# A hybrid decoder trunk on one core: dt's 16 columns leave the unit list, V goes first, the first weights load in halves, and the last unit's split and the final norm weight move forward

## The chip, the cores and the metric

The kernel runs on one core of one Trainium2 chip. The metric is device time in microseconds (us) of one execution; lower is better. Before the change three runs took 965.58 to 969.66 us, median 967.36 us. A change of less than about 0.5% (4.8 us) can't be told from none.

The engines are named as in the profile: PE (TensorE, matrix products), DVE (VectorE), ACT (ScalarE), POOL (GpSimd), SP (SyncE, which here issues nearly all DMAs).

## The reference, cut to what matters

576 tokens (512 of a prompt, 8 sequences of 8 sample tokens) go through two layers of 1024 channels.

```
h    = rmsnorm(x, norm_w)
proj = h @ w_in        # 1024 -> [z 1024 | xBC 1536 | dt 16 | q 512 | k 512 | v 512 | g_ret 512 | u 512 | g_pool 512]
dt   = softplus(dt_raw + dt_bias);  a = -exp(a_log)      # 16 heads
y_ssd  = rmsnorm((ssd(silu(conv(xBC)), dt, a) + x*d_skip) * silu(z))
y_ret  = rmsnorm(retention(rotary(q), rotary(k), v)) * silu(g_ret)
y_pool = pool(u) @ pool_w * pool_scale * silu(g_pool)
x = x + concat(y_ssd, y_ret, y_pool) @ w_out             # 2048 -> 1024
...                                                      # after both layers
y = rmsnorm(x, final_norm_w)
```

The new recurrent states are outputs too. All data are 32-bit floats.

## The kernel before

**Units.** The two projections of a layer are cut into units of 128 output columns. A unit is eight blocks of 128 channels by two halves of 288 tokens by three products (high part of the weights times high and low part of h, low part times high part), so 48 matmuls of 128x288 (`products`, L534 to L536). A layer has 61 units: dt (U_DT = 0, its 16 columns padded with zeros to 128), four each of q, k and v, 12 of conv, 4 pool, 8 gates, 8 z, and 16 of the output projection. The accumulators of two units alternate.

**What a unit needs.** Two units ahead SP loads the raw weights (`load`, L383); ACT writes their high part (`high`, L888), after the unit that used this buffer is projected; DVE subtracts to get the low part (`split`, L1156, semaphore w_split). PE starts a unit when its split is there and the accumulator of the unit two before is read (evac). On ACT and DVE the main loop goes over u and starts each round with the high part, or the split, of unit u+2, so both stand in the queue behind the end of unit u.

**Start of a layer.** x is multiplied with the norm weight and split into high and low (`raw_high`, `raw_low`); the first five units (EARLY) are computed from this, before the root mean square is known, and DVE multiplies them with rstd when it reads them (`read_early`). In the first layer units 0 and 1 run interleaved, four blocks apart, as x arrives (`project_first`). `norm_sum` adds the squares of x over the channels with four plain 32-bit matmuls by a matrix of ones. While units 0 to 3 run DVE and ACT make the scaled h (`scaled`, `half_high`), which later units use.

**dt and rotary on DVE.** dt_raw is read from unit 0 (L1181). In ACT's round 4 come its bias, Abs and Exp (L1063 to L1067); DVE does the rest of softplus and the running sums as `dt_part(0..7)` in rounds 4 to 11 (a RECIPROCAL in part 1), and one q or k unit is rotated in each of rounds 4 to 11 (`rotate`). Part 7 leaves `stacked` (semaphore stk_ok). Behind unit 12 PE transposes it (L862), and DVE copies the result to `token_vecs` in its round 12 (L1611, L1612; semaphore tokv_ok). Retention starts behind unit 13 (`ret_turn`, L691); its first matmuls overwrite the same PSUM banks and wait for tokv_ok.

**The end.** The last two units go half by half (`project_last`), each half with its own final norm: add to x (L1680), square (L1127), sum (L797, L799), rstd (L1134, L1136), and eight SCALAR_TENSOR_TENSOR x * final_norm_w * rstd of 128x288 (`out_of`, L1695). In the last rounds ACT's `high` and DVE's `split` of unit u+2 stand behind the square and the add of round u.

Of the kernel before, what the change touches and what calls it, by code (L numbers as in the profile page):

```python
# [13 lines left out]
P = 128  # L14
# [23 lines left out]
U_DT = 0  # L38
U_Q = 1
U_K = U_Q + RP  # L40
U_V = U_K + RP
U_CONV = U_V + RP
# [7 lines left out]
DT_AT = 4  # L50
# [79 lines left out]
def trunk(nc: bass.Bass, a):  # L130
    with ExitStack() as ctx:
# [69 lines left out]
        stk = place("stacked", [96, TOK])  # L201
        tokv = place("token_vecs", [P, TILES, 96])
        gm = place("scores", [P, GROUPS, CH])
# [54 lines left out]
        tab_in = sem("tables_loaded")  # L258
        vec_in = sem("layer_vectors_loaded", 16)
# [4 lines left out]
        s_st = sem("small_states_loaded", 32)  # L264
        w_hid = sem("w_high", UNITS)
# [94 lines left out]
        sum_half = sem("last_norm_sum")  # L360
        rstd_half = sem("last_norm_rstd")
# [15 lines left out]
        def _(sp):  # L377
# [24 lines left out]
            def beside(l, s):  # L402
# [11 lines left out]
                if s == 9:  # L414
# [5 lines left out]
                if s == 10:  # L420
# [58 lines left out]
            sp.dma_start(vec[:, :], a["vec"][0]).then_inc(vec_in, 16)  # L479
            for i in range(4):  # L480
                sp.dma_start(x[:, 2 * i:2 * i + 2, :], a["x"][:, 2 * i:2 * i + 2, :]).then_inc(s_x[i], 16)
                if i < 2:
                    load(i)
            for l in range(DEPTH):
# [6 lines left out]
                for u in range(UNITS):  # L491
# [8 lines left out]
                    if l + 1 < DEPTH and u == U_OUT + 10:  # L500
                        sp.wait_ge(*of(y_full, KT))
                        sp.dma_start(vec[:, :], a["vec"][l + 1]).then_inc(vec_in, 16)
                    if l + 1 < DEPTH and u in (UNITS - 4, UNITS - 2):
                        keep((u - UNITS + 4) // 2)
                    if l and u in (0, 2):
                        keep(2 + u // 2)
            for half in range(2):
                c = slice(half * HALF, (half + 1) * HALF)
                for i in range(4):
                    sp.wait_ge(f_ok, KT * half + 2 * i + 2)  # L510
# [5 lines left out]
        def _(pe):  # L516
# [20 lines left out]

            def project_first():

                for step in range(KT + LAG):  # L540
                    if step == KT + 2:
                        norm_sum(0)
                    for u, k in ((0, step), (1, step - LAG)):
# [4 lines left out]
                        if k == 0:  # L548
# [6 lines left out]
            def project_again():  # L555

                pe.wait_ge(*of(w_split, 1))
# [226 lines left out]

            def project_last():
# [30 lines left out]
            for l in range(DEPTH):  # L816
# [4 lines left out]
                for u in range(1, UNITS if l + 1 < DEPTH else UNITS - 2):  # L821
# [3 lines left out]
                    if u == S_RST:  # L825
# [27 lines left out]
                    elif u > 1 or l:  # L853
                        project(u)
                    if U_GPOOL < u < U_GPOOL + 4 and (u - S_SSD) % 2 == 1:

                        pool_mm_(u - U_GPOOL - 1)
                    if u == S_STK:
                        pe.wait_ge(*of(tab_in, 16))
                        pe.wait_ge(*of(stk_ok, 1))  # L860
                        for t in range(TILES):
                            mm = pe.transpose(mb[:, t // 4, (t % 4) * 96:(t % 4 + 1) * 96], stk[:, cols(t)] if t < TILES - 1 else gm[0:96, 0, :],  # L862
                                              ident[0:96, 0:96])
                        mm.then_inc(stk_T, 1)
# [12 lines left out]
        def _(eng):  # L877
# [40 lines left out]
            def read_out(u):  # L918

                src = acc_of(whole(l, u))  # L920
                if u < U_V:
# [5 lines left out]
                elif u < U_CONV:  # L927
                    go(act(halves(vT[:, u - U_V, :]), src, ACT.Copy), evac, u + 1)
# [82 lines left out]
            eng.wait_ge(*of(vec_in, 16))  # L1011
            for j in range(KT):
                if j % 2 == 0:
                    eng.wait_ge(*of(s_x[j // 2], 16))
                if j in (1, 4):
                    high(j // 4)
                raw_high(j, 0)
            for j in range(KT):
                if j >= 2:
                    eng.wait_ge(*of(sq_add, j - 1))  # L1020
                square(j, 0)
            for l in range(DEPTH):
                for u in range(UNITS if l + 1 < DEPTH else UNITS - 2):
# [3 lines left out]
                    m = u - U_OUT - OUT_CHUNKS  # L1027
                    if m >= 0:
# [10 lines left out]
                    if whole(l, u) + 2 < DEPTH * UNITS:  # L1039
# [20 lines left out]
                    if u == DT_AT:  # L1060
                        eng.wait_ge(*of(s_par, 48))
                        eng.wait_ge(*of(evac, 1))
# [6 lines left out]
                    if u == 6:  # L1069
# [3 lines left out]
                    if u == 10:  # L1073
# [843 lines left out]
```

## Time and profile before

| | us |
|---|---|
| runs | 965.58, 967.36, 969.66 |
| the profiled execution | 967.27 |
| its span (first to last instruction) | 965.5 |
| PE busy | 947.5 (98%) |
| DVE busy | 693.6 (72%) |
| ACT busy | 419.3 (43%) |
| mean granted TensorE clock | 0.994 of full |

The profile is of one execution. In a row of the timeline the first number is the start, the second the time over which the instructions of the row lie; what stands in brackets is how long the engine was idle before and what released it. A plain 32-bit matmul of the program shows as two MATMUL rows. The starts of matmuls that follow each other show PE's pace; their lengths overlap.

### The profile page before, as it was taken

The page shows a single profiled execution, that of the slowest core. Times are in us where ns is not written, and L with a number is a line of the kernel's source. Part 1 is how long each engine was busy: PE and PEld are TensorE (multiplying, and loading weights), DVE is VectorE, ACT ScalarE, POOL GpSimd, SP SyncE. Part 2 cuts the span into 40 slices and gives each one's busy share as a digit, 9 for nine tenths or more (in the row PEclk, how much of TensorE's full clock was granted, in tenths as well). Part 3 has the DMA queues.
Part 4 walks back from the last instruction along what each step waited for, and adds up shares of the span by engine and source line. Part 5 has one row for each costly group of instructions (what it writes and reads, how often), then busy time and mean ns, then how long its engine had stood idle before and what let it go on. Part 6 is the DMA issues. An engine that isn't in the chain of part 4 may idle for free.

```text
span 965.5 us, 18839 instructions
## 1 busy us (share of the span) xinstructions
PE 947.5 (98%) x7974; PEld 906.6 (94%) x7974; DVE 693.6 (72%) x944; ACT 419.3 (43%) x701; POOL 45.4 (5%) x148
## 2 busy tenths in 40 slices
PE   8999999999999999999999999999999999999996
PEld 7999999999999889999999999999989988899995
DVE  6899677857896568664558967787679757686445
ACT  6432454234775135532334235533267633544222
POOL 0000011010010000000000001011101000000000
PEclk9999999999999999999999999999999999999999
DMA  7234221234234453423333242221533451652222
GB/s 268 104 115 146 81 67 49 69 108 155 88 107 153 153 204 123 142 91 109 132 127 113 87 143 64 67 67 50 157 107 103 136 198 63 224 202 66 88 66 99
DMA packets 38277, 113.33 MB, mean 117 GB/s; under 512 B 11088, under 2 KB 13776, under 8 KB 36784
## 3 DMA queue, kind: packets, MB, share of 16 engines
q1 hardware_dynamic: 37936, 111.23, 34.7%
q8 instruction: 63, 1.03, 0.4%
q0 software_dynamic: 256, 0.88, 0.3%
q14 instruction: 22, 0.18, 0.1%
HBM read 94.63 MB, written 17.47 MB: 116 GB/s over the span
## 4 chain that ended last, share of the span: by engine, by line
PE 90%; DVE 5%; ACT 3%; DMA 1%; issue 1%; SPq 0%; DVEq 0%; ACTq 0%
PE acc L534 26%; PE acc L536 25%; PE acc L535 25%; PE misc L638 2%; PE misc L624 1%; DVE w_lo L1156 1%; ACT w_hi L888 1%; PE misc L691 1%; PE misc L641 1%; DMA x<-in_x 1%; PE misc L713 1%; PE acc L781 1%; PE misc L762 1%; PE misc L732 1%; PE misc L655 1%; PE misc L610 1%
## 5 line engine op out<-in xcount | busy, mean ns | idle before, releaser
L534 PE MATMUL acc<-hin,w_hi 128*128 128x288 f32 x1536 | 461.4, 300 | 0.9 <-DVE w_lo L1156 0.9
L536 PE MATMUL acc<-hin,w_lo 128*128 128x288 f32 x1536 | 453.8, 295 | 0.0
L535 PE MATMUL acc<-hin,w_hi 128*128 128x288 f32 x1536 | 453.7, 295 | 0.0
L534 PEld LDWEIGHTS acc<-hin,w_hi 128*128 128x128 f32 x1536 | 289.5, 188 | 13.6 <-issue 10.8
L888 ACT ACTIVATE w_hi<-w_raw 128x1024 fp32r<-128x1024 f32 x122 | 129.0, 1057 | 381.8 <-PE acc L536 378.6
L535 PEld LDWEIGHTS acc<-hin,w_hi 128*128 128x128 f32 x1536 | 289.5, 188 | 0.4
L536 PEld LDWEIGHTS acc<-hin,w_lo 128*128 128x128 f32 x1536 | 289.5, 188 | 0.0
L1156 DVE TENSOR_TENSOR w_lo<-w_raw,w_hi 128x1024 fp32r<-128x1024 f32 x122 | 148.8, 1220 | 126.5 <-ACT w_hi L888 126.4
L534 PE MATMUL acc<-mix,w_hi 128*128 128x288 f32 x416 | 124.0, 298 | 4.0 <-DVE w_lo L1156 1.7
L536 PE MATMUL acc<-mix,w_lo 128*128 128x288 f32 x416 | 122.6, 295 | 0.0
L535 PE MATMUL acc<-mix,w_hi 128*128 128x288 f32 x416 | 122.5, 294 | 0.0
L534 PEld LDWEIGHTS acc<-mix,w_hi 128*128 128x128 f32 x416 | 78.0, 188 | 4.9 <-issue 3.0
L535 PEld LDWEIGHTS acc<-mix,w_hi 128*128 128x128 f32 x416 | 78.0, 188 | 0.3
L536 PEld LDWEIGHTS acc<-mix,w_lo 128*128 128x128 f32 x416 | 78.1, 188 | 0.0
L1256 DVE SCALAR_TENSOR_TENSOR conv_out<-halo,vec,conv_out 128x600 f32<-128x600 f32 x72 | 60.8, 844 | 2.5
L981 ACT ACTIVATE decay<-decay,token_vecs 128x128 f32<-128x128 f32 (+1 forms) x160 | 47.8, 379 | 1.9
L1587 DVE TENSOR_TENSOR x<-x,acc 128x576 f32<-128x576 f32 x30 | 22.6, 754 | 34.6 <-PE acc L536 32.7
L892 ACT ACTIVATE mix<-x,vec 128x576 fp32r<-128x576 f32 x16 | 11.8, 770 | 38.8 <-DVE x L1587 34.5
L906 ACT ACTIVATE tmp<-x 128x576 f32<-128x576 f32 x22 | 14.8, 678 | 31.8 <-PE acc L536 14.2
L638 PE MATMUL misc<-decay,xdt 128*64 128x128 f32 (+1 forms) x320 | 27.3, 266 | 0.0
L1303 DVE TENSOR_TENSOR xdt<-misc,token_vecs 128x1024 f32<-128x1024 f32 x10 | 12.2, 1224 | 19.1 <-PE misc L615 18.9
L638 PEld LDWEIGHTS misc<-decay,xdt 128*64 128x64 f32 (+1 forms) x320 | 19.4, 136 | 6.8 <-issue 6.8
(212 smaller groups left out, 1045.2 us busy)
## 6 DMA issues: line engine op xcount, KB each, us to landing
w_raw<-in_w SPq DMA_DIRECT2D x122, 512.0 KB, 3.6
decay<-cum_rows SPq DMA_DIRECT2D x8, 1024.0 KB, 6.0
h<-in_ssm SPq DMA_DIRECT2D x16, 512.0 KB, 6.3
out_ssm_s<-h SPq DMA_DIRECT2D x16, 512.0 KB, 6.2
x<-in_x SPq DMA_DIRECT2D x8, 576.0 KB, 6.9
x_kept<-x SPq DMA_DIRECT2D x4, 576.0 KB, 2.8
x<-x_kept SPq DMA_DIRECT2D x4, 576.0 KB, 5.8
out_y<-x SPq DMA_DIRECT2D x8, 288.0 KB, 2.2
```

What stands on the lines that cost most here:

```text
L534: pe.matmul(out, wh, hi, start=k == 0, stop=False)
L535: pe.matmul(out, wh, lo, start=False, stop=False)
L536: return pe.matmul(out, wl, hi, start=False, stop=k == KT - 1)
L638: mm = pe.matmul(dst[r, :], xdt[0:n, h * HD:(h + 1) * HD], decay[0:n, t % 2, h, 0:n], start=True, stop=not inter)
L888: go(act(w_hi[:, unit % 2, :, :], w_raw[:, unit % RAW, :, :], ACT.Copy), w_hid, unit + 1, 0)
L892: go(act(raw_h(0, j), x[:, j, :], ACT.Copy, scale=vec[:, V_NW + j:V_NW + j + 1]), p_hi, j + 1, at)
L906: go(act(tmp[:, j % 2, :], x[:, j, :], ACT.Square), sqd, j + 1, at)
L981: go(act(m, m, ACT.Relu, scale=-1.0, bias=tokv[0:n, t, h:h + 1]))
L1156: go(V.tensor_tensor(w_lo[:, unit % 2, :, :], w_raw[:, unit % RAW, :, :], w_hi[:, unit % 2, :, :].bitcast(F32), ALU.subtract), w_split, un ...
L1256: ins = V.scalar_tensor_tensor(out=o, in0=h[:, c:c + CVO], scalar=w[c], in1=o, op0=ALU.mult, op1=ALU.add)
L1303: go(V.tensor_tensor(heads(xdt[:, :]), src, dt_b, ALU.mult))
L1587: go(V.tensor_tensor(halves(x[:, m, :]), halves(x[:, m, :]), acc_of(whole(l, u)), ALU.add), x_new, o + 1)
```

## The change

- The dt unit goes; a layer has 60 units, V first (units 0 to 3), then q (4 to 7), k (8 to 11), conv from 12. DVE's `read_early` now reads the four v units and the first q unit.
- dt's columns are their own small weights, 8 blocks of 128x32 (`wdt`, in the place of token_vecs), multiplied with the norm weight by one DVE instruction. `dt_parts` multiplies them as plain 32-bit numbers with the raw x, block k into the strip of 32 PSUM partitions k mod 4; ACT copies the four strips out, `dt_folded` adds them with a 0/1 matrix behind unit 2, and DVE scales the result with rstd (`dt_scaled`).
- The dt rounds on ACT and DVE come one round sooner (DT_AT 3 instead of 4; 5 and 9 instead of 6 and 10); rotations stay in rounds 4 to 11, so q or k unit u is now rotated in round u itself.
- `stacked` is turned inside unit 12, after its first three blocks, and retention starts behind unit 12. DVE's copies to token_vecs stay in round 12, behind the split of unit 14.
- In the first layer the first unit's weights load in two halves, and two squares and their adds move ahead of the second unit's high part and split.
- In the last layer the last unit's high part and split come before the x add of unit 57 (the third from the end); ACT multiplies x with the final norm weight as soon as a chunk is done, and DVE's output step is four TENSOR_TENSOR of 128x2x288 per half instead of eight SCALAR_TENSOR_TENSOR of 128x288.

DVE around the token vectors, before (the rotation of the last k unit, part 7 of dt, the split of unit 14, the copies, the split of unit 15, retention):

```order
L1273 TENSOR_TENSOR qk<-qk,conv_out 128x576 [waits vector_order]
L1240 TENSOR_TENSOR stacked<-xbc 16x576 [waits exp_to_end,rotated]
L1242 COPY scores<-stacked 96x128 [waits vector_order]
L1156 TENSOR_TENSOR w_lo<-w_raw,w_hi 128x1024 [waits w_high]
L1611 COPY token_vecs<-misc 128x384 [waits w_split,stacked_turned]
L1612 COPY token_vecs<-misc 128x96
L1156 TENSOR_TENSOR w_lo<-w_raw,w_hi 128x1024 [waits w_high]
L1419 TENSOR_TENSOR ret_probs<-misc,tab 128x1024 [waits w_split,ret_slots_zeroed,ret_turned]
```

and now (part 7, the split of unit 13, the last rotation, the split of unit 14, the copies, retention):

```order
L1327 TENSOR_TENSOR stacked<-xbc 16x576 [waits exp_to_end,rotated]
L1329 COPY scores<-stacked 96x128 [waits vector_order]
L1229 TENSOR_TENSOR w_lo<-w_raw,w_hi 128x1024 [waits w_high]
L1355 STREAM_SHUFFLE conv_out<-qk 128x576 [waits w_split,acc_read]
L1357 TENSOR_TENSOR conv_out<-conv_out,tab 128x576 [waits vector_order]
L1358 TENSOR_TENSOR qk<-qk,tab 128x576
L1360 TENSOR_TENSOR qk<-qk,conv_out 128x576 [waits vector_order]
L1229 TENSOR_TENSOR w_lo<-w_raw,w_hi 128x1024 [waits w_high]
L1712 COPY token_vecs<-misc 128x384 [waits w_split,stacked_turned]
L1713 COPY token_vecs<-misc 128x96
L1506 TENSOR_TENSOR ret_probs<-misc,tab 128x1024 [waits token_vecs_ready,ret_slots_zeroed,ret_turned]
```

Between the copies and retention no split stands any more: the copies and retention's first work are in one round.

DVE from the fourth early read to the reciprocal, before (split of unit 6, early read, first rotation, dt part 0, split of unit 7, second rotation, part 1):

```order
L1156 TENSOR_TENSOR w_lo<-w_raw,w_hi 128x1024 [waits w_high]
L1183 TENSOR_TENSOR qk<-acc,rstd 128x576 [waits w_split,norm_rstd,projected]
L1268 STREAM_SHUFFLE conv_out<-qk 128x576 [waits acc_read]
...
L1205 TENSOR_SCALAR xbc<-xbc 16x576 [waits dt_exp,rotated]
...
L1156 TENSOR_TENSOR w_lo<-w_raw,w_hi 128x1024 [waits w_high]
L1268 STREAM_SHUFFLE conv_out<-qk 128x576 [waits w_split,acc_read]
...
L1212 TENSOR_TENSOR xbc<-xbc 16x576 [waits rotated]
L1213 RECIPROCAL xbc<-xbc 16x576
L1156 TENSOR_TENSOR w_lo<-w_raw,w_hi 128x1024 [waits w_high]
```

and now (the scaled h of round 3, dt part 0, split of unit 6, early read, first rotation, part 1, split of unit 7):

```order
L1282 TENSOR_TENSOR hin<-x,hin 128x576 [waits h_high] x2
L1292 TENSOR_SCALAR xbc<-xbc 16x576 [waits dt_exp,h_split]
...
L1229 TENSOR_TENSOR w_lo<-w_raw,w_hi 128x1024 [waits w_high]
L1254 TENSOR_TENSOR qk<-acc,rstd 128x576 [waits w_split,norm_rstd,projected]
L1355 STREAM_SHUFFLE conv_out<-qk 128x576 [waits acc_read,tables_loaded]
...
L1299 TENSOR_TENSOR xbc<-xbc 16x576 [waits rotated]
L1300 RECIPROCAL xbc<-xbc 16x576
L1229 TENSOR_TENSOR w_lo<-w_raw,w_hi 128x1024 [waits w_high]
```

The split behind the reciprocal was that of unit 8 and is now that of unit 7; one rotation and one split less stand ahead of it.

The core of the diff:

```diff
-U_DT = 0
-U_Q = 1
+U_V = 0
+U_Q = U_V + RP
 U_K = U_Q + RP
-U_V = U_K + RP
-U_CONV = U_V + RP
+U_CONV = U_K + RP
...
-DT_AT = 4
+DT_AT = 3
...
+            sp.dma_start(w_raw[:, 0, first, :], a["w"][0][:, first, :]).then_inc(w0_in, 16)
+            sp.dma_start(wdt_all[:, :], a["wdt"][0]).then_inc(dt_in, 16)
             for i in range(4):
                 sp.dma_start(x[:, 2 * i:2 * i + 2, :], a["x"][:, 2 * i:2 * i + 2, :]).then_inc(s_x[i], 16)
-                if i < 2:
-                    load(i)
+                if i == 0:
+                    sp.dma_start(w_raw[:, 0, rest, :], a["w"][0][:, rest, :]).then_inc(s_raw[0], 16)
+                if i == 1:
+                    load(1)
...
+            def dt_parts(first, end):
+                for half in range(2):
+                    for k in range(first, end):
+                        if half == 0 and l:
+                            pe.wait_ge(*of(x_new, OUT_CHUNKS + k + 1, l - 1))
+                        elif half == 0 and k % 2 == 0:
+                            pe.wait_ge(*of(s_x[k // 2], 16))
+                        r = strip(k % 4)
+                        mm = pe.matmul(mb[r, half, 0:HALF], wdt[:, k, :], halves(x[:, k, :])[:, half, :],
+                                       start=k < 4, stop=k >= 4)
+                if end == KT:
+                    mm.then_inc(dt_sum, 1)
+
+            def dt_folded():
+                pe.wait_ge(*of(dt_part_ok, 1))
+                for half in range(2):
+                    mm = pe.matmul(mb[0:HEADS, half, 0:HALF], fold, halves(cvt[:, 0, 0:TOK])[:, half, :],
+                                   start=True, stop=True)
+                mm.then_inc(dt_fold, 1)
...                                                    # project_first
+                pe.wait_ge(*of(dt_w_ok, 1))
+                dt_parts(0, 2)
                 for step in range(KT + LAG):
                     if step == KT + 2:
+                        dt_parts(2, KT)
                         norm_sum(0)
...                                                    # project_again
+                pe.wait_ge(*of(dt_w_ok, 1))
+                dt_parts(0, KT - 1)
+                dt_parts(KT - 1, KT)
...                                                    # PE's units
+                    if u == S_RET:
+                        project(u, stacked_turn, 2)
...
+                    if u == 2:
+                        dt_folded()
...                                                    # ACT, start
+            go(act(w_hi[:, 0, 0:KT // 2, :], w_raw[:, 0, 0:KT // 2, :], ACT.Copy), w0_hi, 1)
             for j in range(KT):
+                if j == 2:
+                    eng.wait_ge(*of(s_raw[0], 16))
+                    go(act(w_hi[:, 0, KT // 2:KT, :], w_raw[:, 0, KT // 2:KT, :], ACT.Copy), w_hid, 1, 0)
+                if j == 4:
+                    square(0, 0)
+                    square(1, 0)
+                    high(1)
...                                                    # ACT, rounds
+                    ahead = l == DEPTH - 1 and u == UNITS - 3
+                    if ahead:
+                        high(whole(l, u) + 2)
...
+                        if l + 1 == DEPTH:
+                            settle()
+                            go(act(x[:, m, :], x[:, m, :], ACT.Copy, scale=T("fnw")[:, m:m + 1]))
+                    if u == 0:
+                        eng.wait_ge(*of(dt_sum, 1))
+                        go(act(halves(cvt[:, 0, 0:TOK]), mb[:, 0:2, 0:HALF], ACT.Copy), dt_part_ok, 1)
...                                                    # DVE, rounds
+                    ahead = o < OUT_CHUNKS or l == DEPTH - 1 and u == UNITS - 3
+                    if ahead and whole(l, u) + 2 < DEPTH * UNITS:
                         split(whole(l, u) + 2)
...
-                    if U_Q + 3 <= u < U_V + 3:
-                        rotate(u - U_Q - 3)
+                    if U_Q <= u < U_CONV:
+                        rotate(u - U_Q)
+                    if u == 2:
+                        dt_scaled()
...
-                    if u == S_STK:
+                    if u == S_RET:
                         eng.wait_ge(*of(stk_T, 1))
...                                                    # DVE, the end
-            out_of(0, 5, 0)
+            out_of(0, 2, 0)
             x_of(KT - 1, 1)
-            out_of(5, KT, 0)
-            out_of(0, KT, 1)
+            out_of(2, 4, 0)
+            out_of(0, 4, 1)
```

## Rows read from the trace of the kernel before

**Rows 1.** The page's busy times, with the share of the span.
```profile
PE 947.5 (98%) x7974; PEld 906.6 (94%) x7974; DVE 693.6 (72%) x944; ACT 419.3 (43%) x701; POOL 45.4 (5%) x148
```
**Rows 2.** PE's waits: us in total, times, longest us.
```profile
PE acc L534 <- DVE w_lo L1156: 2.6, 2, 1.7
...
PE acc L534 <- DVE mix L1162: 1.4, 1, 1.4
...
PE misc L862 <- DVE scores L1242: 1.1, 2, 0.5
```
**Rows 3.** Timeline of PE at `norm_sum`, first layer: start us, us, engine, line.
```profile
22.83 1.13 PE L595 MATMUL misc<-ssq,ones 128*128 128x288 f32 x4
23.80 1.13 PE L598 MATMUL misc<-tmp,ones 128*128 128x288 f32 x4
...
27.41 0.37 PE L534 MATMUL acc<-mix,w_hi 128*128 128x288 f32 x1 [0.90 <-DVE xbc L1181]
```
**Rows 4.** Chain of work at the sample states' 32-column matmuls: start us, us.
```profile
316.95 1.85 PE misc L655 x16
```
**Rows 5.** Timeline of ACT, start of the first layer, and dt.
```profile
7.47 1.06 ACT L888 ACTIVATE w_hi<-w_raw 128x1024 fp32r<-128x1024 f32 x1 [0.41 <-DMA w_raw<-in_w]
...
11.63 1.06 ACT L888 ACTIVATE w_hi<-w_raw 128x1024 fp32r<-128x1024 f32 x1 [1.10 <-DMA x<-in_x]
...
15.27 1.24 ACT L906 ACTIVATE tmp<-x 128x576 f32<-128x576 f32 x2
...
47.80 0.76 ACT L1063 ACTIVATE xbc<-xbc,head_vec 16x576 f32<-16x576 f32 x1
...
49.31 0.69 ACT L1067 ACTIVATE xbc<-xbc 16x576 f32<-16x576 f32 x1
```
**Rows 6.** Timeline of PE: unit 8 starts, unit 12 ends, retention starts; later the last matmul.
```profile
65.66 0.29 PE L534 MATMUL acc<-hin,w_hi 128*128 128x288 f32 x1
...
97.32 0.29 PE L536 MATMUL acc<-hin,w_lo 128*128 128x288 f32 x1
...
105.05 1.16 PE L691 MATMUL misc<-qk 64*128 64x128 f32 x16
...
957.49 0.75 PE L799 MATMUL misc<-tmp,ones 128*128 128x288 f32 x2 [1.20 <-ACT tmp L1127]
```
**Rows 7.** Timeline of DVE, first layer: a rotation, the split behind the reciprocal, the copies.
```profile
47.93 1.23 DVE L1156 TENSOR_TENSOR w_lo<-w_raw,w_hi 128x1024 fp32r<-128x1024 f32 x1 [1.14 <-ACT w_hi L888]
...
50.19 0.81 DVE L1268 STREAM_SHUFFLE conv_out<-qk 128x576 f32<-128x576 f32 x1
...
53.30 0.45 DVE L1205 TENSOR_SCALAR xbc<-xbc 16x576 f32<-16x576 f32 x1
...
63.79 1.15 DVE L1156 TENSOR_TENSOR w_lo<-w_raw,w_hi 128x1024 fp32r<-128x1024 f32 x1
...
98.80 1.22 DVE L1156 TENSOR_TENSOR w_lo<-w_raw,w_hi 128x1024 fp32r<-128x1024 f32 x1 [0.81 <-ACT w_hi L888]
...
100.60 0.25 DVE L1612 COPY token_vecs<-misc 128x96 f32<-128x96 f32 x1
```
**Rows 8.** Timeline of DVE, the end.
```profile
942.77 0.76 DVE L1172 TENSOR_TENSOR ssq<-ssq,tmp 128x576 f32<-128x576 f32 x1 [1.08 <-ACT tmp L906]
...
954.16 2.23 DVE L1695 SCALAR_TENSOR_TENSOR x<-x,tab,rstd 128x288 f32<-128x288 f32 x5
956.50 0.45 DVE L1680 TENSOR_TENSOR x<-x,acc 128x288 f32<-128x288 f32 x1
...
959.28 3.52 DVE L1695 SCALAR_TENSOR_TENSOR x<-x,tab,rstd 128x288 f32<-128x288 f32 x8 [0.85 <-ACT rstd L1136]
```
**Rows 9.** Stretches: us, busy PE (x), PEld, DVE, ACT, POOL; PEclk, DMA share, GB/s.
```profile
2.00:4.00 2.00, 2.00 (x10) 2.00 (x11) 0.00 (x0) 0.02 (x1) 0.00 (x0) 1.00 0.86 200
...
6.00:8.00 2.00, 2.00 (x20) 2.00 (x19) 0.80 (x1) 1.30 (x2) 0.00 (x0) 1.00 1.01 413
...
961.20:961.40 0.20, 0.00 (x0) 0.00 (x0) 0.20 (x1) 0.00 (x0) 0.00 (x0) 0.52 1.02 374
```

More of the change, by code:

```diff
@@ L201, in trunk @@
         stk = place("stacked", [96, TOK])
+        tokv_at = top[0]
         tokv = place("token_vecs", [P, TILES, 96])
+        wdt_all = place("w_dt", [P, KT * DT_W + HEADS], at=tokv_at)
+        wdt = wdt_all[:, 0:KT * DT_W].rearrange("p (k n) -> p k n", k=KT)
+        fold = wdt_all[:, KT * DT_W:]
         gm = place("scores", [P, GROUPS, CH])
@@ L783, in pool_mm_, with stacked_turn @@
                 mm.then_inc(pool_mm, 1)
+            def stacked_turn():
+                pe.wait_ge(*of(tab_in, 16))
+                pe.wait_ge(*of(stk_ok, 1))
+                for t in range(TILES):
+                    src = stk[:, cols(t)] if t < TILES - 1 else gm[0:96, 0, :]
+                    mm = pe.transpose(mb[:, t // 4, (t % 4) * 96:(t % 4 + 1) * 96], src, ident[0:96, 0:96])
+                mm.then_inc(stk_T, 1)
             def project_last():
@@ L1036, in _ @@
                         square(m, l + 1)
+                        if l + 1 == DEPTH:
[4 more added lines that the diff above has]
+                        go(act(halves(cvt[:, 0, 0:TOK]), mb[:, 0:2, 0:HALF], ACT.Copy), dt_part_ok, 1)
                     if u == 0 and l:
                         norm_rstd(l)
-                    if whole(l, u) + 2 < DEPTH * UNITS:
+                    if whole(l, u) + 2 < DEPTH * UNITS and not ahead:
                         high(whole(l, u) + 2)
@@ L1128, in square_half @@
                    sq_half, 2 * half + m - (KT - 2) + 1)
+                settle()
+                go(act(halves(x[:, m, :])[:, half, :], halves(x[:, m, :])[:, half, :], ACT.Copy,
+                       scale=T("fnw")[:, m:m + 1]), x_weighted, 2 * half + m - (KT - 2) + 1)
             def rstd_of(half):
@@ L1564, in _ @@
             settle()
[L1565 removed]
+            eng.wait_ge(w0_hi, 1)
+            go(V.tensor_tensor(w_lo[:, 0, 0:KT // 2, :], w_raw[:, 0, 0:KT // 2, :],
+                               w_hi[:, 0, 0:KT // 2, :].bitcast(F32), ALU.subtract), w0_lo, 1)
+            dt_weights(0)
             for j in range(KT):
[L1567 to L1568 removed]
+                if j == 2:
+                    eng.wait_ge(*of(w_hid, 1, 0))
+                    go(V.tensor_tensor(w_lo[:, 0, KT // 2:KT, :], w_raw[:, 0, KT // 2:KT, :],
+                                       w_hi[:, 0, KT // 2:KT, :].bitcast(F32), ALU.subtract), w_split, 1, 0)
+                if j == 4:
+                    add_square(0, 0)
+                    add_square(1, 0)
+                    split(1)
                 raw_low(j, 0)
[L1570 removed]
+            for j in range(2, KT - 1):
                 add_square(j, 0)
@@ L1593, in _ @@
                                 add_square(m, l + 1)
-                            if whole(l, u) + 2 < DEPTH * UNITS:
+                            if not ahead and whole(l, u) + 2 < DEPTH * UNITS:
                                 split(whole(l, u) + 2)
+                    if u == UNITS - 4 and l + 1 < DEPTH:
+                        dt_weights(l + 1)
                     if u < EARLY:
@@ L1691, in out_of @@
                 eng.wait_ge(rstd_half, half + 1)
+                eng.wait_ge(x_weighted, 2 * half + 2)
                 settle()
-                for j in range(first, end):
-                    xh = halves(x[:, j, :])[:, half, :]
-                    go(V.scalar_tensor_tensor(out=xh, in0=xh, scalar=T("fnw")[:, j:j + 1],
-                                              in1=halves(rstd[:, :])[:, half, :], op0=ALU.mult, op1=ALU.mult),
-                       f_ok, KT * half + j + 1)
+                r = halves(rstd[:, :])[:, half, :].unsqueeze(1).to_broadcast([P, 2, HALF])
+                for i in range(first, end):
+                    two = x[:, 2 * i:2 * i + 2, half * HALF:(half + 1) * HALF]
+                    go(V.tensor_tensor(two, two, r, ALU.mult), f_ok, 4 * half + i + 1)
             x_of(KT - 2, 0)
```

83 lines of the change are left out of this document (48 added, 35 removed).

## The prediction

> **What bounds the kernel now.** I read the busy times first: PE works 98% of the span [rows 1], so an edit is worth what it takes off PE or out of PE's waits, and costs what it puts there. Second, PE's own waits [rows 2], which are few: 1.7 and 0.9 us (together the 2.6) for a weight split at the start and at the end, 1.4 us at the start for h's low part, 0.5 us in each layer for `stacked`. Third, the timelines around the places that the change touches, to see who is late there. DVE is, in each layer's first twelve units: the split behind the reciprocal starts at 63.79 without any idle time ahead of it, ends at 64.94, and PE begins the unit that it belongs to at 65.66 [rows 6, 7]. So there are 0.7 us of slack at the tightest place.
>
> **The change part by part.** All sums are made against the profiled execution, 967.27 us, 0.1 us from the median of the three runs (967.36).
>
> *The dt unit goes.* Unit 2 starts at 27.41 [rows 3], unit 8 at 65.66 [rows 6]: 38.25 us for six units, 6.37 us each, 0.13 us per matmul. Two units are 12.7 us off PE.
>
> *The strips come.* No row has a plain 32-column matmul of 288 tokens. From above: two plain 128-column matmuls of this length take 0.97 us (22.83 to 23.80 [rows 3]), 0.485 each; if the strips ran one after the other, the first layer's 12 that stand inside the stream would cost 5.8 us and the second layer's 16 7.8 us. From below: the sample states' 8 matmuls of 512 columns into four strips take 1.85 us [rows 4], so each strip worked off two in that time, 0.93 us per round of 512, 0.52 us per round of 288; were all strips always full, 28 matmuls would take 3.6 us. I take the row on strips, since it is the same kind of instruction, with the strips counted: in the first layer blocks 2 to 7 give strips 2 and 3 four matmuls each, four rounds, 2.1 us; in the second the last block's two both go to strip 3 after all others, five rounds, 2.6 us. Together +4.7 us (3.6 to 13.6). The first layer's first four matmuls lie at the start, where PE waits for h anyway. The two folds are plain matmuls of full price: 2 x 0.97 = +1.9 us.
>
> *DVE comes earlier to the dt chain, PE still earlier to its split.* With one unit less and a fold more PE reaches the critical unit (now unit 7) 6.4 - 1.0 = 5.4 us sooner after the first early read. DVE loses ahead of the reciprocal one rotation (50.19 to 53.30, 3.1 us) and one split with its gap (1.3 us), and gains `dt_scaled`, at the price of an instruction of 576 columns 0.8 us [rows 7, 8]. Its idle time changes too: the 1.1 us before the split of unit 6 [rows 7] are filled, but part 0 now follows the scaled h directly and waits for ACT's bias, Abs and Exp, 47.80 to 50.00 = 2.2 us [rows 5], of which only DVE's last subtraction of about 0.7 us covers any: 1.5 us of new idling. DVE is therefore 3.1 + 1.3 - 0.8 - 0.4 = 3.2 us sooner, PE 5.4, and with 0.7 us of slack PE waits 1.5 us for the split of unit 7; adding the small idle times that also fill up I take 1.4, in both layers, since the second has the same instructions: +2.8 us (0 to 5). Later splits catch up by the rounds without dt work.
>
> *Token vectors: the new wait.* PE now needs them right behind unit 12, and DVE's copies stand behind the split of unit 14, which waits for ACT's high part, which waits for the end of unit 12. That chain is in the trace, only that PE then had unit 13 to do: last matmul of unit 12 at 97.32 [rows 6], split at 98.80 with idle time ahead that ACT's high part ended, copies done at 100.85 [rows 7]. Retention began at 105.05 [rows 6], 4.2 us after the copies, and waited for nothing. Now PE would have to wait 100.85 - 97.32 - 0.13 = 3.4 us per layer: +6.8 us (0 to 8). What is queued behind the waiting matmul is the whole retention, so nothing of PE's moves under it, and PE has no later waits of size in which it could be given back [rows 2].
>
> *Stacked inside unit 12.* Its wait of 2 x 0.5 us goes [rows 2]: part 7 stands as before one split and one rotation behind the end of a unit, and PE now does 9 of 48 matmuls, 1.2 us, before it asks. -1.1 us (-1.1 to +1).
>
> *The start.* x's first part has 0.40 MB of weights ahead of it, at 413 GB/s [rows 9] 1.0 us; ACT's wait of 0.4 us for the first weights goes, and half a high part (0.5 us); then two squares, 1.24 us, stand ahead of the second high part, which had 1.1 us of idle time in that place [rows 5]. 1.0 - 0.4 - 0.5 + 1.2 - 1.1 = +0.2 us, and DVE's two adds follow in the same shadow: I take +0.3 us (-1.5 to +2). PE's first matmul does come sooner, but the wait of 1.4 us at the fifth block [rows 2] grows by as much, because ACT's second high part ends it in both.
>
> *The end.* The last unit's split leaves the chain; in its place PE waits for x of unit 57, which now stands behind high part, split and add: 1.06 + 1.2 + 0.8 and gaps, 3.3 us after that unit's end, when PE has worked 3.2 us on the next half. Of 0.9 us, 0.8 are gained. The last x add stands behind five output instructions (954.16 to 956.39 [rows 8]) and starts at 956.50; with two of 576 columns ahead, about 1.5 us, it comes 0.7 us sooner, which the last sum's wait of 1.2 us [rows 6] can give. The last outputs, eight in 3.52 us, become four at 0.76 us or a little less in a row [rows 8], 2.9 us: 0.6. Sum -2.1 us (-2.6 to -0.5).
>
> *At nothing:* V first as such (DVE has five early reads in both), ACT's copy of the strips (0.7 us under the squares' sum of 1.9), the weighting of dt's weights (a short DVE instruction while x loads, and among the first layer's last units, where DVE waits for PE), ACT's final weights (0.7 us per unit of 6.4), two more DMA issues on SP ahead of x, and one per layer later. If the copy's cover were gone, 0.7 us per layer.
>
> Sum: -12.7 + 4.7 + 1.9 + 2.8 + 6.8 - 1.1 + 0.3 - 2.1 = +0.6 us, **967.9 us**: what the unit gives, dt's own matmuls and two new waits take back.
>
> **The rivals.**
> *The token vectors are not waited for* (or wait behind something that ends as early). For it: `stacked` is turned 1.8 us into unit 12, so the copies' input is there 4.5 us before the unit ends. Against: DVE works in order, and the order shows a split with its wait ahead of the copies. 967.9 - 6.8 = 961.1 us, faster.
> *The clock falls in the new waits; slower.* The last matmul ended at 958.24 [rows 6] and at 961.2 the granted clock stood at 0.52 [rows 9], so 3.0 us of idling were enough there to go from 2.4 to 1.2 GHz; the token waits are 3.4 us, longer than any wait of PE inside the program so far (1.7 us [rows 2]). At the lower level PE does half: in the warm-up 10 matmul rows in 2 us against 20 later [rows 9]; the switch lies between 4 and 6, 2.3 to 4.3 us after the first. A fall would cost half of such a stretch, 1.2 to 2.2 us, 1.7 in each layer: 971.3 us; were a whole unit run at half pace in both, 6.4 us each, 980.7 us. It decides from the clock falling before retention's matmuls begin. Against it: the 3.0 us at the end followed on a wait of 1.2 us and one short matmul [rows 6], these waits follow on a dense unit. The Trainium skill, TensorE: Matmul & The Clock Gate, section "What's actually happening", has it that the throttled state is the default and activity releases it, which is the same mechanism, and by it the longer time; the trace agrees as far as its two ends go (10 against 20 rows at the start, 0.52 at the end).
> *The strips run one after the other.* Then they cost 13.6 instead of 4.7 us: 976.8 us. Against it stands the 1.85 us row [rows 4], for it only that the blocks here differ in weights and x at once.
>
> **How the numbers follow.** Forecast 0.62, own range 964.5 to 970.5 (the two waits half as long or half as long again, the end as bounded). No token wait 0.14, clock falls 0.17, strips in a row 0.07. Range: from 960.5, to hold the first rival, to 972.5, which holds the second with its usual price; the third and the dear end of the second are left out, some 0.13. Less than 0.5%, 4.8 us, can't be told from no change. Faster (below 962.5): the first rival and a tail of the forecast in which both waits are much shorter, 0.18. Slower (above 972.2): the third, a third of the second, 0.14. Same: 0.68.
>
> **What would show it.** In PE's waits: retention's first matmul (L741) on DVE's token copy, twice about 3.4 us; unit 7's first matmul on a split, 1 to 2 us per layer; no wait of L841. In PE's timeline: 12 and 16 strip matmuls in about 2.1 and 2.6 us. In DVE's timeline: idling of 1.5 us before part 0 of dt. At the end: the last x add directly behind PE's last matmul, the last outputs in under 3 us. In the stretches behind the token waits: a granted clock of 1.00, or below for the second rival. I am wrong if PE does not stand still behind unit 12, or if the strips take the time of full matmuls.

## The result and the profile after

Five runs of the changed kernel took 975.06 to 977.40 us, median 976.39, against 967.36 before: 9.0 us more, a ratio of 1.0092 with a 95% interval of 1.0076 to 1.0108. The forecast was 967.9 us and its range ended at 972.5; the measured time lies 3.9 us above it.

The profiled execution took 976.73 us (before 967.27), 9.5 us more. Its busy times, which answer to [rows 1]:

```profile
PE 950.4 (97%) x7950; PEld 903.8 (93%) x7950; DVE 692.0 (71%) x939; ACT 424.0 (43%) x710; POOL 43.5 (4%) x148
```

PE has 24 matmul rows fewer and is yet busy 2.9 us longer, so part of the loss is not waiting: some of the work ran more slowly. PE's waits, against [rows 2]:

```profile
PE misc L741 <- DVE token_vecs L1713: 6.8, 2, 3.4
PE acc L554 <- DVE mix L1235: 2.8, 2, 2.2
PE acc L554 <- DVE w_lo L1229: 2.7, 2, 1.4
...
PE acc L554 <- DVE x L1684: 0.3, 1, 0.3
```

The two token waits, the two waits for unit 7's split and the 0.3 us at the end are about as forecast, and no wait of L841 is left. The wait at the start was 1.4 us and is now 2.2; the forecast let it grow, but put the block behind it only 0.3 us later.

PE's timeline behind the token wait (start, us; in brackets the idle time ahead and what ended it); before, the same 16 rows took 1.16 us [rows 6]:

```profile
105.64 0.29 PE L556 MATMUL acc<-hin,w_lo 128*128 128x288 f32 x1
109.32 2.08 PE L741 MATMUL misc<-qk 64*128 64x128 f32 x16 [3.38 <-DVE token_vecs L1713]
```

The stretches there have the granted clock behind POOL's busy time (columns as in [rows 9]):

```profile
108.00:108.50 0.50, 0.00 (x0) 0.00 (x0) 0.40 (x2) 0.00 (x0) 0.50 (x2) 0.74 0.00 0
108.50:110.50 2.00, 1.18 (x10) 1.21 (x12) 0.68 (x2) 0.00 (x0) 0.04 (x1) 0.50 0.52 123
...
112.50:115.00 2.50, 2.50 (x12) 2.50 (x11) 1.66 (x2) 1.55 (x5) 0.00 (x0) 0.50 0.00 0
115.00:115.50 0.50, 0.50 (x5) 0.50 (x5) 0.47 (x2) 0.33 (x2) 0.00 (x0) 0.94 0.00 0
```

The clock went from 2.4 to 1.2 GHz inside the wait, while PE stood still, and came back only at about 115.1. From 109.32 on PE worked at half pace: (115.0 - 109.32) / 2 = 2.8 us lost, 2.9 with the tail. In the second layer retention starts at 583.85 (5.15 us at 0.50 and a tail: 2.8 us lost):

```profile
583.00:589.00 6.00, 5.15 (x30) 4.96 (x31) 1.84 (x3) 1.02 (x3) 0.07 (x1) 0.50 0.24 87
589.00:590.00 1.00, 1.00 (x8) 1.00 (x7) 0.96 (x3) 0.86 (x3) 0.00 (x0) 0.74 0.00 0
```

A third fall lies behind the longer wait at the start (0.5 + 1.0 + 0.2 = 1.7 us lost):

```profile
16.00:17.00 1.00, 1.00 (x5) 1.00 (x6) 1.00 (x2) 1.00 (x3) 0.00 (x0) 0.54 0.84 139
17.00:19.00 2.00, 2.00 (x10) 2.00 (x10) 1.84 (x3) 0.61 (x3) 0.00 (x0) 0.50 1.07 393
19.00:20.00 1.00, 1.00 (x8) 1.00 (x7) 0.85 (x2) 0.82 (x2) 0.00 (x0) 0.76 0.97 414
```

So the 9.5 us are: 0.6 as forecast, 7.4 of half clock behind three waits, 0.9 by which the fifth block came later than forecast, and 0.6 that I can't place. Both kernels also have a fall behind 64 small matmuls of retention in each layer (in the kernel before, 0.50 from 190 to 192 us); the three are on top of these. The lower clock is not peculiar to the profiled execution: all five runs have a mean granted clock of 0.986 to 0.988, where the profiled execution before has 0.994, and 0.008 of 975 us is 7.8 us (an estimate, near the 7.4).

### The profile page after: what moved, and what is told of

Same layout as the page of the kernel before. It is cut to its first block, busy times and chain, and to the rows that moved or that the text cites. A ratio compares the mean times of both kernels' runs of the same rounds, so it can differ in the third digit from the quotient of the medians.

```text
span 974.8 us, 18802 instructions
## 1 busy us (share of the span) xinstructions
PE 950.4 (97%) x7950; PEld 903.8 (93%) x7950; DVE 692.0 (71%) x939; ACT 424.0 (43%) x710; POOL 43.5 (4%) x148
## 4 chain that ended last, share of the span: by engine, by line
PE 85%; DVE 8%; ACT 5%; issue 1%; DMA 1%; SPq 0%; DVEq 0%; ACTq 0%
PE acc L554 24%; PE acc L556 23%; PE acc L555 23%; DVE w_lo L1229 2%; ACT w_hi L944 1%; PE misc L688 1%; ACT decay L1035 1%; PE misc L741 1%; PE misc L674 1%; PE misc L763 1%; PE acc L831 1%; PE misc L812 1%; ACT decay L1042 1%; PE misc L782 1%; PE misc L705 1%
## 5 line engine op out<-in xcount | busy, mean ns | idle before, releaser
L554 PE MATMUL acc<-hin,w_hi 128*128 128x288 f32 x1504 | 453.3, 301 | 3.0 <-DVE w_lo L1229 2.7
L555 PE MATMUL acc<-hin,w_hi 128*128 128x288 f32 x1504 | 445.1, 296 | 0.0
L556 PE MATMUL acc<-hin,w_lo 128*128 128x288 f32 x1504 | 444.9, 296 | 0.0
L554 PEld LDWEIGHTS acc<-hin,w_hi 128*128 128x128 f32 x1504 | 284.3, 189 | 16.1 <-issue 11.3
L944 ACT ACTIVATE w_hi<-w_raw 128x1024 fp32r<-128x1024 f32 x119 | 125.8, 1057 | 379.1 <-PE acc L556 377.2
L555 PEld LDWEIGHTS acc<-hin,w_hi 128*128 128x128 f32 x1504 | 284.5, 189 | 0.4
L556 PEld LDWEIGHTS acc<-hin,w_lo 128*128 128x128 f32 x1504 | 284.4, 189 | 0.0
L1229 DVE TENSOR_TENSOR w_lo<-w_raw,w_hi 128x1024 fp32r<-128x1024 f32 x119 | 145.2, 1220 | 134.5 <-ACT w_hi L944 134.3
L948 ACT ACTIVATE mix<-x,vec 128x576 fp32r<-128x576 f32 x16 | 11.9, 770 | 37.7 <-DVE x L1684 34.5
```

Source lines behind the costliest of these rows:

```text
L554: pe.matmul(out, wh, hi, start=k == 0, stop=False)
L555: pe.matmul(out, wh, lo, start=False, stop=False)
L556: return pe.matmul(out, wl, hi, start=False, stop=k == KT - 1)
L944: go(act(w_hi[:, unit % 2, :, :], w_raw[:, unit % RAW, :, :], ACT.Copy), w_hid, unit + 1, 0)
L948: go(act(raw_h(0, j), x[:, j, :], ACT.Copy, scale=vec[:, V_NW + j:V_NW + j + 1]), p_hi, j + 1, at)
L1229: go(V.tensor_tensor(w_lo[:, unit % 2, :, :], w_raw[:, unit % RAW, :, :], w_hi[:, unit % 2, :, :].bitcast(F32), ALU.subtract), w_split, un ...
```

## The experiments

Twelve kernels were run. Each is compared with runs of the kernel before on the same chip (medians 966.5 to 967.0 us). "The clock falls" means from 1.00 to 0.50 of 2.4 GHz in the rows.

**1. Token copies ahead of the split** (`copies_first`). DVE's two copies no longer stand behind a split that waits for the end of unit 12:

```diff
+                    if u == S_RET:
+                        ...                     # wait for stk_T, both copies to token_vecs
                     ahead = o < OUT_CHUNKS or l == DEPTH - 1 and u == UNITS - 3
                     if ahead and whole(l, u) + 2 < DEPTH * UNITS:
                         split(whole(l, u) + 2)
...
-                    if u == S_RET:              # the same lines, behind the split
```

> The changed kernel with DVE's two token-vector copies moved ahead of the split of unit 14 in the same round. Theory A (PE's 3.4 us wait behind unit 12, and the fall of the granted clock that it brings, 2.8 us more, in both layers): 976.4 - 2 x 6.2 = 964 us, the clock stays at 1.00 behind unit 12. Theory B (only the wait costs; the lower clock is made up elsewhere): 976.4 - 6.8 = 969.6 us.

964.27 us (963.64 to 965.28, 6 runs), ratio 0.9971 [0.9956, 0.9985]. That is 12.1 us less than the changed kernel, where the waits themselves are 6.8; no wait of L741 is left. The other 5.3 us fit the half clock behind them, which the trace put at 5.7. In the one profiled execution, the slowest of the six, a part comes back: the fall behind retention's small matmuls lasts 6.8 us in the second layer, against 3.4 in the changed kernel.

**2. The token wait filled** (`warm_wait`). The wait stays, but PE multiplies a matrix of ones in it:

```diff
+                    if u == S_RET:
+                        for i in range(15):
+                            pe.matmul(mb[:, 2 + i % 2, 0:P], ones, ones, start=True, stop=True)
```

> The changed kernel with 15 plain matmuls of a matrix of ones by itself (128 columns, about 0.21 us each, 3.2 us) on PE between unit 12 and retention, so that PE works through the wait; the wait for the token vectors itself stays. Theory A: the clock does not fall, retention begins as late as before, 976.4 - 5.6 = 970.8 us. Theory B: 976.4 us, no change.

971.23 us (969.38 to 972.06, 5 runs), ratio 1.0037 [1.0021, 1.0053]: work that nobody needs makes the kernel 5.2 us shorter. Retention starts at 109.22 (109.32 in the changed kernel), and then has its old pace. This kernel's PE timeline, and below it the stretch, with a granted clock of 1.00:

```profile
109.22 1.16 PE L741 MATMUL misc<-qk 64*128 64x128 f32 x16
```
```profile
108.00:110.00 2.00, 1.97 (x25) 1.80 (x25) 0.97 (x3) 0.00 (x0) 0.43 (x2) 1.00 0.23 49
```

This separates the two: the clock behind the waits costs 5.2 us, and the waits alone 7.0 (971.23 - 964.27, two kernels in whose profiles no clock falls at the token vectors; 6.8 in the trace).

**3. The start's wait filled** (`warm_start`): nine such matmuls ahead of the fifth block.

```diff
+                    if step == LAG:
+                        for i in range(9):
+                            pe.matmul(mb[:, 2 + i % 2, 0:P], ones, ones, start=True, stop=True)
```

> The changed kernel with 9 such matmuls ahead of the fifth block of the first unit, where PE idles 2.2 us. Theory A (this idle time lets the clock fall, 3.6 us at half pace behind it): the clock stays, 976.4 - 1.8 = 974.6 us. Theory B: 976.4 us.

974.22 us (973.35 to 974.65, 4 runs), ratio 1.0067 [1.0050, 1.0084]: 2.2 us less, as expected. The clock stays at 1.00 from 14 to 18 us.

The token waits are those of the changed kernel here, twice 3.38 us. Behind the first the clock fell, behind the second it did not. The second layer's retention in PE's timeline, and the stretches of the wait:

```profile
582.40 1.16 PE L744 MATMUL misc<-qk 64*128 64x128 f32 x16 [3.38 <-DVE token_vecs L1716]
```
```profile
580.00:582.00 2.00, 0.00 (x0) 0.00 (x0) 1.69 (x2) 0.83 (x4) 0.72 (x2) 1.00 0.00 0
582.00:584.00 2.00, 1.60 (x21) 1.51 (x22) 0.25 (x2) 0.00 (x0) 0.00 (x0) 1.00 0.62 197
```

**4. The old start** (`old_start`): weights in whole units, squares last, all 16 strip matmuls ahead of the squares' sum.

```diff
-            sp.dma_start(w_raw[:, 0, first, :], ...)      # and the second half
...
+                if i < 2:
+                    load(i)
...
-                dt_parts(0, 2)
...
-                        dt_parts(2, KT)
...
+                        dt_parts(0, KT)
...                                                    # the squares' place
```

> The changed kernel with the first layer's start as before the change: whole first weights, squares behind all of h's parts, all 16 strip matmuls ahead of the squares' sum. Theory A: PE waits 1.4 us instead of 2.2 us at the fifth block, which then begins 1.2 us sooner, and the clock does not fall there: -1.2 - 1.8 + 0.5 for the four strip matmuls that now stand in the stream, 973.9 us. Theory B (clock without effect): 975.7 us. Theory C (the new start is worth what it says): slower than 976.4 us.

973.37 us (972.99 to 973.65, 4 runs), ratio 1.0058 [1.0039, 1.0077]: the new start costs 3.0 us. Here the fifth block waits 1.36 us and the clock does not fall; the 16 strip matmuls in one piece take 2.15 us, no more than the 12.

**5. The same token wait in the kernel before** (`before_wait`): its copies one round later, behind the split of unit 15.

```diff
-                    if u == S_STK:
+                    if u == S_RET:
                         eng.wait_ge(*of(stk_T, 1))
```

> The kernel before with one thing moved: DVE's token-vector copies from round 12 to round 13, behind the split of unit 15, so that retention, which there starts behind unit 13, must wait for them as it does in the changed kernel. Theory A (such a wait costs itself and lets the clock fall, whatever kernel it stands in): 3.4 + 2.8 us in each layer, 967.0 + 12.4 = 979.4 us, granted clock 0.5 behind both waits. Theory B (only the wait): 973.8 us.

978.21 us (977.64 to 978.91, 4 runs), ratio 1.0121 [1.0095, 1.0147]. The time is near theory A's, 11.6 us for 6.8 us of waits, but not all of it by theory A's way. The waits are 3.38 us in each layer. In the second layer the clock falls behind it. In the first it does not: PE stands still from 106.35 to 109.73, and in the stretches of this kernel the first two rows have 1.00. Instead the fall behind retention's small matmuls (the other two rows) lasts about 6.8 us in place of 3.4:

```profile
107.00:109.00 2.00, 0.00 (x0) 0.00 (x0) 1.37 (x2) 1.16 (x4) 0.72 (x2) 1.00 0.00 0
109.00:112.00 3.00, 2.27 (x26) 2.18 (x27) 0.63 (x3) 0.05 (x1) 0.00 (x0) 1.00 0.51 180
192.00:194.00 2.00, 2.00 (x66) 2.00 (x66) 1.93 (x3) 0.00 (x0) 0.00 (x0) 0.86 0.27 63
...
198.00:200.00 2.00, 2.00 (x11) 2.00 (x10) 0.15 (x1) 0.00 (x0) 0.00 (x0) 0.50 0.00 0
```

In this profile the start's wait was 2.0 us, though nothing was changed there, and the clock fell behind it too. So of three new stretches at half clock (1.7 us of lost pace each) only one stands behind a token wait, and a wait of a given length brings a fall in one place and none in another.

**6. dt one round later** (`late_dt`), to free the split of unit 7: DT_AT 4 again, and part 7 behind part 5 without the empty round between them, so that it stays in round 10.

```diff
-DT_AT = 3
+DT_AT = 4
...
-                elif k == 7:
+                elif k == 6:
```

> The changed kernel with dt's rounds on ACT and DVE one later again (the reciprocal behind the split of unit 7), and part 7 directly behind part 5's round so that stacked is ready as before. Theory A: PE's wait of 1.4 us for the split of unit 7 goes in both layers, DVE's idling before part 0 too, 976.4 - 2.7 = 973.7 us; the token wait stays. Rival: DVE's work only moves, the wait appears at another split or at the turn of stacked (L841), 976 us.

980.22 us (979.36 to 981.72, 4 runs), ratio 1.0146 [1.0115, 1.0177]: 3.8 us more than the changed kernel, so theory A fell. The waits for unit 7's split go (2.7 us), and PE waits inside unit 12 for `stacked` instead. From PE's waits of this kernel:

```profile
PE misc L841 <- DVE scores L1329: 4.9, 2, 2.5
```

ACT's Exp of the running sums (L1144) stays in its round 9, while the sums now come one round later: ACT stands idle for 7.4 us until they come, the high part behind the Exp is late, and DVE idles 1.7 us ahead of the split of unit 12. Of the 3.8 us, 2.2 are the waits. In the two profiled executions, 2.9 us apart, another 1.1 us is half clock (an estimate from PE's busy time in the stretches at 0.50: 11.9 against 10.8 us of lost pace).

This kernel has the changed kernel's start and its 2.16 us wait, and in its profile the clock did not fall there. The fifth block, and the stretches around it:

```profile
15.81 0.40 PE L554 MATMUL acc<-mix,w_hi 128*128 128x288 f32 x1 [2.16 <-DVE mix L1235]
```
```profile
14.00:16.00 2.00, 0.19 (x1) 0.19 (x2) 2.00 (x3) 2.00 (x4) 0.00 (x0) 1.00 0.42 165
16.00:18.00 2.00, 2.00 (x16) 2.00 (x16) 1.95 (x3) 1.47 (x3) 0.00 (x0) 1.00 1.03 287
```

**7. The end alone** (`end_only`): the kernel before with the change's last part only (the last unit's high part and split sooner, the final weight on ACT, four outputs per half instead of eight).

```diff
+                    ahead = l == DEPTH - 1 and u == UNITS - 3
+                    if ahead:
+                        high(whole(l, u) + 2)
...
+                            go(act(x[:, m, :], x[:, m, :], ACT.Copy, scale=T("fnw")[:, m:m + 1]))
...
-            out_of(0, 5, 0)
+            out_of(0, 2, 0)
```

> The kernel before with the change's last part alone (the last unit's split sooner, final norm weight on ACT, wide output instructions). My sum has -2.1 us for it: 964.9 us. Rival (the outputs' DMAs end last anyway): no change, 967 us.

964.59 us (962.91 to 965.65, 12 runs), ratio 0.9977 [0.9964, 0.9989]: 2.1 us, as forecast for this part (1.1 to 3.5 by the interval).

**8. and 9. All three together** (`best1`: edits 1, 4 and 6; `best2`: also `stacked` turned eight blocks later in unit 12).

```diff
-                        project(u, stacked_turn, 2)
+                        project(u, stacked_turn, 10)      # best2 only
```

> The changed kernel with the copies first, the old start and the late dt rounds together. Theory A: the three gains add, as they stand in different stretches: 976.4 - 12.1 - 3.0 - 2.7 = 958.6 us, clock at 1.00 throughout behind the start. Rival (waits take each other's place): 961 to 964 us.

> All three repairs at once (token copies ahead of the split of unit 14, the old start of the first layer, dt one round later), and the turning of `stacked` behind the 11th block of unit 12 instead of the 3rd, 3.2 us later. Theory A (the waits are the only cost: best1's wait of 2.5 us per layer at the turning goes, and with it the halved clock behind it): 965.2 - 4.9 - about 1 = 959.3 us (958 to 961), no wait of L832 and none at retention's first matmul, mean clock at least 0.995. Rival B (the later turning makes the copies late again, so that retention waits for them): 962 to 966 us and a wait at retention's first matmul.

965.16 us (961.59 to 967.36, 12 runs; ratio 0.9982 [0.9966, 0.9998]) and 964.91 us (963.14 to 965.81, 12 runs; 0.9979 [0.9968, 0.9991]). Theory A fell in both. In `best1` the wait at L832 is that of experiment 6. In `best2` it goes, and the copies are late again, 2.0 us in each layer, now behind the last rotation. Of these rows of DVE's timeline the first is the split of unit 12, the second ends the last rotation:

```profile
92.26 1.22 DVE L1214 TENSOR_TENSOR w_lo<-w_raw,w_hi 128x1024 fp32r<-128x1024 f32 x1 [1.70 <-ACT w_hi L935]
...
101.29 0.76 DVE L1345 TENSOR_TENSOR qk<-qk,conv_out 128x576 f32<-128x576 f32 x1
102.15 0.56 DVE L1655 COPY token_vecs<-misc 128x384 f32<-128x384 f32 x1
102.63 0.25 DVE L1656 COPY token_vecs<-misc 128x96 f32<-128x96 f32 x1
```

PE stood still from 101.02 to 103.02, and here the clock fell only after it had begun again, in the stretches of `best2`:

```profile
103.00:104.00 1.00, 0.98 (x16) 0.99 (x16) 0.00 (x0) 0.00 (x0) 0.00 (x0) 1.00 0.22 90
104.00:105.00 1.00, 1.00 (x8) 0.83 (x5) 0.00 (x0) 0.73 (x1) 0.00 (x0) 0.50 0.17 70
```

So what is freed at unit 7 is missing at unit 12. That DVE has too much to do for dt to come later is not shown by this: in both kernels it idles 1.7 us ahead of the split of unit 12, because ACT's Exp was left in round 9 (experiment 6), and no run moved the Exp too.

**10. Copies first and the old start** (`best3`: edits 1 and 4, dt as in the change).

> Token copies first and the old start, dt rounds as in the change. Theory A (costs add: copies first takes 12.1 us off the changed kernel, the old start 3.0): 976.4 - 12.1 - 3.0 = 961.3 us (960 to 962.8), with the waits of 1.4 us for the split of unit 7 still there. Rival B (the two overlap, since the halved clock at the start only moves to another wait): 964 us.

962.29 us (960.76 to 962.70, 6 runs), ratio 0.9947 [0.9930, 0.9963]. Theory A: the costs add. In its profile, the fastest of the six runs, no clock falls at the start or at the token copies, nor behind retention's small matmuls in the first layer; the other five have a mean clock of 0.993 instead of 0.995 and take 1.4 to 1.9 us longer.

**11. Copies first, the start's wait filled** (`cf_warm`: edits 1 and 3).

> Token copies first, and nine extra 128-column matmuls of the ones matrix ahead of the fifth block of the first layer (dummy work into a free bank, its results are read by nobody). Theory A (gains add: 12.1 and 2.2 us): 976.4 - 14.3 = 962.1 us (961 to 963.5). Rival B (without the token waits the start's fall is given back later, so that filling it gains nothing): 964.3 us.

963.63 us (962.02 to 965.91, 12 runs), ratio 0.9960 [0.9948, 0.9971]. Between the two theories and inconclusive: the clock holds at the start, unit 2 begins 1.4 us sooner than in experiment 1 (30.34 against 31.78 in the two timelines), but the medians are only 0.6 us apart.

**12. Copies first, squares late** (`sq_late`): edit 1, the weights in halves as in the change, and the two squares and their adds back behind the last raw split.

```diff
                 if j == 4:
-                    square(0, 0)
-                    square(1, 0)
                     high(1)
...
                 if j == 4:
-                    add_square(0, 0)
-                    add_square(1, 0)
                     split(1)
```

> Token copies first, the first unit's weights in halves as in the change, but the two squares and their two adds again behind the last raw split, as before the change. Theory A (the squares ahead of the second high part made the wait of 2.2 us at the fifth block, and that wait the halved clock): ACT's second high part 1.1 us sooner, the wait about 1.0 us, the clock of the start stays at 1.00, and so 1.1 + 1.8 = 2.9 us less than token copies first alone: 964.3 - 2.9 = 961.4 us (960.4 to 962.6). Rival B (the halved weights ahead of x delay x's blocks and are what makes the wait): the wait stays near 2 us, the clock falls at the start, 963.5 to 965 us.

962.46 us (960.93 to 962.90, 6 runs), ratio 0.9947 [0.9933, 0.9960]: theory A. The fifth block now waits 0.25 us, begins at 13.98 instead of 15.34 in experiment 1, and the clock stays at 1.00. The halved weights are thus neither the harm nor a gain: unit 2 begins at 28.94 in this profile, at 28.77 with whole units in `best3`. The harm at the start was the place of the two squares and their adds.

## Why the prediction was wrong

**Clock, the step that failed.** The forecast rested on "these waits follow on a dense unit" as the reason why the clock would hold, and the second rival, "the clock falls in the new waits; slower", got 0.17. It was the right one. Inside the program the clock fell in both token waits, with dense work up to 105.64; the 3.0 us at the end, which I had discounted, were the better guide. Experiments 1 and 2 show it from two sides: filling the waits gives 5.2 us back, removing them 12.1. The rival was likely rather than certain: in the profiles of five kernels eight of ten such 3.38 us waits brought a fall. The rival's price was also low: 1.7 us per layer were worked out from the warm-up's switch, 2.8 and 2.9 were measured, since the low clock lasted to 115.1 and not only through retention's first matmuls. At the measured price the rival would have stood at 967.9 + 2.9 + 2.8 = 973.6 us, already outside the range.

The Trainium skill, TensorE: Matmul & The Clock Gate, section "HAM oscillation — how this bites in real kernels", tells of a matmul kernel that starts cold behind each wait for its data, and advises to reorder its loop so that PE stays warm. The 16 rows at 2.08 us behind the token wait, and 1.16 with the copies first or the wait filled, agree; the 1.16 behind the same wait in the second layer of experiment 3 do not.

**The start, a term mis-sized.** I let the two squares lie in 1.1 us of idle time ahead of ACT's second high part. ACT's timeline after (the first row before the change began at 11.63 [rows 5]):

```profile
11.59 1.24 ACT L962 ACTIVATE tmp<-x 128x576 f32<-128x576 f32 x2
12.73 1.04 ACT L944 ACTIVATE w_hi<-w_raw 128x1024 fp32r<-128x1024 f32 x1
```

PE's fifth block, after, and before:

```profile
15.95 0.51 PE L554 MATMUL acc<-mix,w_hi 128*128 128x288 f32 x1 [2.16 <-DVE mix L1235]
```
```profile
14.74 0.40 PE L534 MATMUL acc<-mix,w_hi 128*128 128x288 f32 x1 [1.38 <-DVE mix L1162]
```

The high part is 1.1 us later and the block 1.2, where +0.3 was forecast. That idle time was a wait for x in the old order, and x's data no longer stood ahead of the high part in the new one; in experiment 12, with the squares gone from there, it begins at 10.90, against 12.13 in experiment 1, where x came within 0.1 us of the same time. Behind the 2.2 us wait that came of it stands the third fall; experiment 3, with the wait filled, gives it back, though experiment 6 shows that the same wait can pass without one. I had weighed the clock only for the token waits.

**What was right.** The strips and folds, PE's timeline:

```profile
25.65 2.13 PE L567 MATMUL misc<-x,w_dt 128*32 128x288 f32 x24
...
38.94 1.14 PE L576 MATMUL misc<-conv_out,w_dt 128*16 128x288 f32 x4
...
490.16 2.17 PE L567 MATMUL misc<-x,w_dt 128*32 128x288 f32 x32
```

2.1 and 2.6 us were forecast for the strips. The first is met. The second was 0.4 us too high: it counted the last block's two matmuls as a fifth round, but strip 3 has four matmuls in all, as the others have. The rival of strips in a row (5.8 and 7.8 us) is out.

DVE's timeline has the idle time before part 0 of dt (1.5 forecast) and the chain that makes the token wait (split, copies):

```profile
54.45 0.45 DVE L1292 TENSOR_SCALAR xbc<-xbc 16x576 f32<-16x576 f32 x1 [1.41 <-ACT xbc L1136]
...
107.13 1.23 DVE L1229 TENSOR_TENSOR w_lo<-w_raw,w_hi 128x1024 fp32r<-128x1024 f32 x1 [2.37 <-ACT w_hi L944]
...
108.93 0.25 DVE L1713 COPY token_vecs<-misc 128x96 f32<-128x96 f32 x1
```

Token wait 3.4 us forecast, 3.38 measured; unit 7's split 1.4 forecast, 1.36 and 1.34 measured; `stacked` no longer waited for. The end's 2.1 us were measured alone in experiment 7; the last outputs after, four against the eight in 3.52 us of [rows 8]:

```profile
969.02 2.77 DVE L1798 TENSOR_TENSOR x<-x,rstd 128x576 f32<-128x576 f32 x4 [0.77 <-ACT rstd L1208]
```

So the idea of the change is good: with the copies, the squares and their adds in other places (experiment 12) it is 4.5 us faster than before instead of 9.0 slower.

## What to carry to other kernels

A new wait of TensorE is to be priced as the wait and the clock behind it: here 6.8 us of waits cost 12.1. Where a wait can't be removed, spare matmuls in it can pay (5.2 us here); where a producer can be put ahead of an instruction that waits for something else, that is better by far (12.1 us, two copies moved). One profile shows one execution: whether a wait brought a fall in it is not yet whether it does so every time. Idle time ahead of an instruction is only free for a moved step if what ends the idle time still stands ahead of it in the new order.

## What the runs showed of the hardware

The granted clock did not follow the length of a wait alone. In the profiles of all fourteen kernels none of the six waits of 1.34 to 1.38 us at the fifth block brought a fall. Of 21 waits of 2.0 to 3.4 us (at the fifth block, at the turn of `stacked`, at the token vectors) 17 did, inside the wait or less than 2 us behind it; in `best2` the clock fell 1.0 us after PE had resumed. Four did not: 3.38 us in the first layer of `before_wait` and in the second of `warm_start`, 2.48 us in the first layer of `best1`, and 2.16 us at the start of `late_dt`, where the same instructions had brought a fall in the changed kernel.

The price differed too. Behind token waits of 3.38 us the lost pace was between 1.7 us (first layer of `old_start`, half clock from 105.6 to 109.0) and 3.2 us (its second layer, to 586.8), or nothing. The fall behind retention's small matmuls, which PE reaches without a long wait, lasted 3.4 or 6.8 us, and in the first layer of `best3` and `sq_late` it was missing. Executions of one kernel differ in this: 23 runs of the kernel before on one chip have mean granted clocks of 0.996 to 0.989 and take 964.7 to 971.3 us, the slowest with the lowest clock. What decides it was not settled; no experiment moved the same wait by small steps in time.

Plain 32-bit matmuls of 32 columns and 288 tokens took 2.13 us for twelve, with four of them in each of the two fullest of the four strips, and 2.15 to 2.17 us for sixteen, with four in each strip. The total did not set the time; four rounds of about 0.53 us, as many as the fullest strip has matmuls, fit all three.
